# Up weights by column halves, down weights by column quarters, an earlier first release and a shared last norm in a decoder block with 32 experts

## What is computed

```python
x = x + mix @ w_o                       # mix: two attention branches, gated
h = rms_norm(x, norm_ffn_g)
logits = h @ w_router + b_router        # top 4 of 32 experts for each token
g = minimum(h @ w_gate[e] + b_gate[e], 7)
u = clip(h @ w_up[e] + b_up[e], -7, 7)
y += gate * (((u + 1) * g * sigmoid(1.702 * g)) @ w_down[e] + b_down[e])
out = rms_norm(x + y, norm_final_g)
```

## Time and profile before

| | us |
|---|---|
| median of 3 runs (1133.7 to 1134.16) | 1133.88 |
| the profiled execution, its time | 1134.85 |
| the profiled execution, its span | 1133.1 |
| PE busy in it | 1071.8 (95%) |
| DVE, ACT busy | 211.1, 133.4 |
| DMA: 438.16 MB, mean rate | 387 GB/s |
| mean granted clock of TensorE | 0.991 |

### The profile page before, as it was taken

The page is one execution under the profiler, slowest core; times in us unless marked ns, Lnnn a source line. Parts: engine busy times, 40 slices in busy tenths (PEclk is TensorE's granted clock), DMA queues, the critical chain, the costliest instruction groups (busy, mean ns, idle before and its releaser), DMA issues.

```text
span 1133.1 us, 11796 instructions
## 1 busy us (share of the span) xinstructions
PE 1071.8 (95%) x5017; PEld 496.6 (44%) x5017; DVE 211.1 (19%) x507; ACT 133.4 (12%) x227; POOL 7.8 (1%) x17
## 2 busy tenths in 40 slices
PE   9999999999999999999999898989898979998886
PEld 8676888643443434344334332433233324332322
DVE  4132143131211120202021201020202020202021
ACT  1112260110010001000100010001000100010002
POOL 1000000000000000000000000000000000000000
PEclk9999999999999999999999999999999999999998
DMA  9982354599999999999999999999999999999995
GB/s 348 426 326 76 149 223 175 234 372 429 413 425 439 430 426 435 433 427 436 433 427 436 433 427 435 434 427 435 433 428 435 433 428 435 433 422 429 426 429 232
DMA packets 26510, 438.16 MB, mean 387 GB/s; under 512 B 4976, under 2 KB 6256, under 8 KB 8560
## 3 DMA queue, kind: packets, MB, share of 16 engines
q1 hardware_dynamic: 26336, 437.67, 91.2%
q10 hardware_dynamic: 144, 0.07, 0.0%
HBM read 436.28 MB, written 1.05 MB: 386 GB/s over the span
## 4 chain that ended last, share of the span: by engine, by line
PE 63%; DMA 35%; ACT 1%; another core or an unknown queue 1%; issue 0%; DVE 0%; ACTq 0%; DVEq 0%; SPq 0%; POOL 0%; POOLq 0%
DMA ring<-in_experts 35%; PE ps L1492 24%; PE ps L1538 11%; PE ps L1160 9%; PE ps L1408 3%; PE ps L1303 2%; PE ps L1151 2%; PE ps L1547 2%; PE ps L1177 1%; PE ps L1351 1%; PE ps L1348 1%; PE ps L1527 1%; PE ps L1417 1%; ACT region_va L666 0%; PE ps L1194 0%
## 5 line engine op out<-in xcount | busy, mean ns | idle before, releaser
L1492 PE MATMUL ps<-ring,xT 128*64 128x512 f32 x2048 | 458.2, 602 | 26.5 <-DMA ring<-in_experts 26.4
L1492 PEld LDWEIGHTS ps<-ring,xT 128*64 128x64 f32 x2048 | 143.7, 138 | 314.9 <-issue 280.3
L1538 PE MATMUL ps<-ring,region_va 128*64 128x512 f32 x1024 | 229.8, 599 | 25.3 <-DMA ring<-in_experts 13.8
L1538 PEld LDWEIGHTS ps<-ring,region_va 128*64 128x64 f32 x1024 | 73.6, 137 | 159.9 <-issue 126.6
L1160 PE MATMUL ps<-ring 128*128 128x256 f32 x448 | 98.5, 380 | 0.0
L1160 PEld LDWEIGHTS ps<-ring 128*128 128x128 f32 x448 | 84.6, 190 | 12.3 <-issue 0.8
L1056 DVE TENSOR_SCALAR g<-ps 128x1024 f32<-128x1024 f32 x16 | 19.6, 1224 | 349.8 <-PE ps L1492 349.8
L1408 PEld LDWEIGHTS ps<-sel,x 128*128 128x128 f32 x480 | 55.4, 192 | 9.5 <-issue 9.5
L1547 PE MATMUL ps<-g,g_T 128*128 128x512 f32 x128 | 59.2, 605 | 0.0
L1408 PE MATMUL ps<-sel,x 128*128 128x128 f32 x480 | 56.7, 276 | 0.0
L1003 DVE TENSOR_TENSOR xT<-ps,g_ffn 128x512 f32<-128x512 f32 x30 | 20.8, 692 | 193.0 <-PE ps L1408 193.0
(11 more groups left out here) (204 smaller groups left out, 446.8 us busy)
## 6 DMA issues: line engine op xcount, KB each, us to landing
ring<-in_experts SPq DMA_DIRECT2D x72, 4096.0 KB, 46.2
ring<-in_experts SPq DMA_DIRECT2D x41, 2048.0 KB, 47.7
ring<-in_head SPq DMA_DIRECT2D x13, 2048.0 KB, 16.0
ring<-in_experts SPq DMA_DIRECT2D x14, 1024.0 KB, 8.2
ring<-in_first SPq DMA_DIRECT2D x7, 384.0 KB, 6.2
x<-in_x SPq DMA_DIRECT2D x2, 512.0 KB, 24.7
out<-x SPq DMA_DIRECT2D x4, 256.0 KB, 2.7
ring<-in_norm_final_g SPq DMA_DIRECT2D x1, 512.0 KB, 13.0
```

What stands on the lines that cost most here:

```text
L1492: last = mm(bank(banks + half)[rows, :], xT[:, 2 * m + c, rows], w[:, c, k, half * W512:(half + 1) * W512], start=False, stop=m == 3 and c ...
L1538: last = mm(bank(first + half)[rows, :], hTm[:, 2 * m + c, rows], w[:, c, k, half * W512:(half + 1) * W512], start=m == 0 and c == 0, stop ...
```

## The change

**Up** loads now hold four chunks of the contraction and half the columns: 4 and 5 are the left half, 6 and 7 the right half. `up_half` goes. The first transposes move from after the last up load to before it, and those of the gates to after load 4.

**Down** loads hold all eight chunks and a quarter of the columns. `down` multiplies by 256 columns; copies and scatters go by quarters (four copies of 256 columns, eight scatter matmuls of 256), each some loads behind its quarter. In an even pair the gather is cut in two by the last scatter. `down_done` goes.

**Early releases.** w_o's right half is laid out as two column quarters, and the left half of slot 5 is loaded when the first of them has been used (`early_left`). Load 0 of pair 1 starts with a quarter, released after the first column half of chunk 0 (`early_quarter`). Gather chunk 3 moves from before gate load 0 into its middle. Gate loads are laid out by chunk and column half.

**Last load** of all: three quarters and one quarter, in place of two halves.

**Last norm.** Both left halves are added, squared and summed and multiplied by the gain on DVE, before the last scatter; then the right halves: squares and roots on ACT, the rest on DVE. POOL scales the left half of token half 0, ACT that of half 1, which ACT also stores. The table of the root is loaded before the last copies. Three stores: 512 KB and twice 256 KB.

```diff
@@ SP: last load, first releases
+LAST_COL = 3 * SLOT_COLS // 4
-                for c, loaded in enumerate((last_rows, unit_loaded[UNITS - 1])):
+                for lo, hi, loaded in ((0, LAST_COL, last_rows), (LAST_COL, SLOT_COLS, unit_loaded[UNITS - 1])):
...
-                                sp_.wait_ge(first_rows_used, p + 1)
-                                load_columns(row, p, 0, SLOT_COLS // 2, early_half[p])
+                                if p == 0:
+                                    sp_.wait_ge(first_rows_used, 1)
+                                    load_columns(row, p, 0, SLOT_COLS // 4, early_quarter)
+                                sp_.wait_ge(first_rows_used, p + 2)
+                                load_columns(row, p, 0 if p else SLOT_COLS // 4, SLOT_COLS // 2, early_half[p])
...
+                if SLOT_OF[p] == 5:
+                    sp_.wait_ge(wo_done, 3)
+                    load_columns(p // 2, p, 0, SLOT_COLS // 2, early_left)
+                    sp_.wait_ge(wo_done, 4)
+                    load_columns(p // 2, p, SLOT_COLS // 2, SLOT_COLS, slot_loaded[5])
+                    continue
@@ ACT: copies by quarters
-                    for b in range(2):
...
-                        nc.scalar.copy(o_s[:, b * W512:(b + 1) * W512], bank(first + b)).then_inc(o_ready, 1)
+                    if closing and q == PAIRS_PER_ITER - 1:
+                        load_root_table()
+                    for j in range(4):
+                        act.wait_ge(load_used, it * LOADS_PER_ITER + LOADS_PER_PAIR * (q + 1) + 9 + j)
+                        nc.scalar.copy(o_s[:, j * T:(j + 1) * T], bank(first + j % 2)[:, (j // 2) * T:(j // 2 + 1) * T]
+                                       ).then_inc(o_ready, 1)
@@ PE: one pair
+                    for m in range(4):
+                        gate(m)
+                    biases(q, 1, second)
+                    up(0, 0)
+                    transpose_gates()
+                    up(0, 1)
+                    up(1, 0)
                     transpose_hidden(0)
+                    up(1, 1)
+
+                    pe.wait_ge(gt_ready, n + 1)
+                    if q == 1 and not last_pair:
+                        pe.wait_ge(sel_ready, n + 2)
+                        gather(first, range(KC))
+
+                    w = down_weights(0)
+                    pe.wait_ge(hT_ready, n * 2 + 1)
                     if q == 1 and not last_pair:
                         pe.wait_ge(xT_ready, n * 2 + 4)
+                    down(0, w, (0, 1))
+                    if q == 1:
+                        transpose_hidden(1)
+                    down(0, w, (2, 3))
+                    if q == 0:
+                        transpose_hidden(1)
+                    pe.wait_ge(hT_ready, n * 2 + 2)
+                    down(0, w, range(4, KC)).then_inc(load_used, 1)
                     if last_pair:
+                        scatter(0)
+                    w = down_weights(1)
+                    down(1, w, range(KC)).then_inc(load_used, 1)
+                    if last_pair:
+                        scatter(1)
+                    else:
+                        scatter(0)
+                    w = down_weights(2)
+                    down(2, w, range(KC)).then_inc(load_used, 1)
+                    if not last_pair:
+                        scatter(1)
+                    w = down_weights(3)
+                    if last_pair:
+                        down(3, w, range(6))
                         pe.wait_ge(unit_loaded[UNITS - 1], (n + 1) * 16)
+                        down(3, w, range(6, KC)).then_inc(load_used, 1)
                     else:
+                        down(3, w, range(KC)).then_inc(load_used, 1)
+                    scatter(2)
                     if q == 0:
+                        pe.wait_ge(sel_ready, n + 2)
+                        gather(first, range(4))
+                        scatter(3)
+                        gather(first, range(4, KC))
+                    else:
+                        scatter(3)
@@ DVE, POOL, ACT: last norm
+            for a in range(NT):
+                add_experts(a, 0)
+            for a in range(NT):
+                left_squares(a)
...
+            for a in range(NT):
+                nc.vector.tensor_tensor(xg[:, a, :], x3[:, a, 0:W512], gfin[:, 0:W512], ALU.mult).then_inc(fin_g, 1)
+            for a in range(NT):
+                add_experts(a, 1)
...
+            nc.gpsimd.tensor_scalar(x3[:, 0, 0:W512], xg[:, 0, :], rstd[:, 0:1], None, ALU.mult).then_inc(fin_left0, 1)
...
+            nc.scalar.activation(x3[:, 1, 0:W512], xg[:, 1, :], ACT.Copy, scale=rstd[:, 1:2]).then_inc(fin_left1, 1)
+            act.wait_ge(fin_left1, 1)
+            act.dma_start(out_d[P:T, 0:W512], x3[:, 1, 0:W512]).then_inc(stored, 16)
```

More of the change, by code:

```diff
@@ L500, in _ @@
             assert own.n == 5
[L502 to L506 removed]
+            pool.wait_ge(fin_g, 1)
+            pool.wait_ge(rstd_ready, 1)
+            nc.gpsimd.tensor_scalar(x3[:, 0, 0:W512], xg[:, 0, :], rstd[:, 0:1], None, ALU.mult).then_inc(fin_left0, 1)
         @block.scalar
@@ L681, in _ @@
+            rounds_after_first(act, expert_iteration, closing=load_root_table)
             for a in range(NT):
[L682 to L686 removed]
@@ L690, in _ @@
                                      bias=fin_bias[:, a:a + 1]).then_inc(fin_std, 1)
-            act.wait_ge(rstd_ready, 1)
-            for half in range(2):
-                cols = slice(half * W512, (half + 1) * W512)
-                act.wait_ge(fin_g, half + 1)
-                nc.scalar.activation(x3[:, 0, cols], xg[:, cols], ACT.Copy,
-                                     scale=rstd[:, 0:1]).then_inc(fin_done0, 1)
+            act.wait_ge(fin_g, 2)
+            act.wait_ge(rstd_ready, 2)
@@ L1497, in gate_or_up @@
-                                if first_pair and 4 * which + m < HALVED and (c, half) == (0, 1):
-                                    last.then_inc(first_rows_used, 1)
-                            last.then_inc(load_used, 1)
-                            if which == 1 and m == 1:
-                                transpose_gates()
+                                    last = mm(bank(first + half)[rows, :], xT[:, 2 * m + c, rows], w[:, c, half, k, :],
+                                              start=False, stop=m == 3 and c == 1, skip_group_check=True)
@@ new lines, in gate, with up @@
+                                if first_pair and c == 0 and (half == 1 or m == 0):
+                                    last.then_inc(first_rows_used, 1)
+                        last.then_inc(load_used, 1)
+                    def up(half, side):
+                        m = 4 + 2 * half + side
+                        w = loaded(m).rearrange("p (c k n) -> p c k n", c=4, k=2)
+                        for c in range(4):
+                            for k in range(2):
+                                rows = slice(k * SLOTS, (k + 1) * SLOTS)
+                                last = mm(bank(second + half)[rows, :], xT[:, 4 * side + c, rows], w[:, c, k, :],
+                                          start=False, stop=side == 1 and c == 3, skip_group_check=True)
+                            if first_pair and m < HALVED and c == 1:
+                                last.then_inc(first_rows_used, 1)
+                        last.then_inc(load_used, 1)
@@ L1510, in expert_iteration @@
                     pe.wait_ge(oh_ready, n + 1)
-                    def gather_next():
-                        pe.wait_ge(sel_ready, n + 2)
-                        gather(first, range(KC))
-                    gate_or_up(0, first)
-                    gate_or_up(1, second)
-                    pe.wait_ge(gt_ready, n + 1)
-                    if q == 1 and not last_pair:
-                        gather_next()
                     def transpose_hidden(b):
@@ L1529, in transpose_hidden, with down @@
                         last.then_inc(ht_done, 1)
-                    transpose_hidden(0)
+                    def down(j, w, chunks):
+                        out = bank(first + j % 2)[:, (j // 2) * T:(j // 2 + 1) * T]
+                        for c in chunks:
+                            for k in range(2):
+                                rows = slice(k * SLOTS, (k + 1) * SLOTS)
+                                last = mm(out[rows, :], hTm[:, c, rows], w[:, c, k, :], start=c == 0, stop=c == KC - 1,
+                                          skip_group_check=True)
+                        return last
@@ L1532, in expert_iteration @@
+                    w = down_weights(0)
+                    pe.wait_ge(hT_ready, n * 2 + 1)
                     if q == 1 and not last_pair:
                         pe.wait_ge(xT_ready, n * 2 + 4)
-                    def down(w, m, half, c):
-                        for k in range(2):
-                            rows = slice(k * SLOTS, (k + 1) * SLOTS)
-                            last = mm(bank(first + half)[rows, :], hTm[:, 2 * m + c, rows],
```

(7 more changed lines are left out.)

231 lines of the change are left out of this document (99 added, 132 removed).

## The result

| us | before | after |
|---|---|---|
| median of 17 runs each | 1134.08 | 1136.89 |
| ratio | | 1.0024 [1.0018, 1.0031] |
| profiled execution: time, span | 1134.85, 1133.1 | 1136.68, 1134.9 |

The kernel became slower by 2.8 us (2.0 to 3.5), a little over the bound of 0.2% that the prediction set for no change. I had forecast 1132.9, so the error is 4.0 us.

What follows compares the result with a forecast made beforehand. The prediction took the DMA weight stream as the bound, leaving its start at the 297.26 us issue and what follows its last byte. Terms +0.4 - 1.8 + 0.5 = -0.9 us from 1133.88 gave 1132.9, range 1131.0 to 1135.0.

Steps and rivals of the forecast that it cites:

- the pinned issue: Weight load issued at 297.26 us, when PE has used pair 1's first two loads; claimed to fix the stream's start.
- T: Landing of the last weight load, 1119.5 us before the change; forecast within 1 us of 1119.9.
- The early releases at 0 for the stream: Head: loading slot 5's left half and a quarter load sooner gains nothing, since PE's path holds the later issue.
- In steady state even +3 us a pair would stay under: Expert loop: 3 us more PE work a pair stays hidden under the stream's 58.4 us.
- +0.4 us for the stream's start: PE's path up to the issue at 297.26 us grows by 0.4 us, bounds -0.5 and +1.4, delaying the stream equally.
- E' = T+4.2: Tail: PE's last scatter ends 4.2 us after the last landing instead of 6.0, saving 1.8 us.
- My rival of landings that fall differently: Stream's end: code fetches miss the last loads, the last landing comes 1.4 to 1.5 us sooner, 1131.4; chance 0.17.
- +0.5: Last norm and stores: the span ends 8.1 us after the last scatter instead of 7.6; bounds -0.3 and +0.9.
- The clock in the tail: Rival: half-speed PE clock after 1109 us is no longer hidden by a wait, costing 1.6 us: 1134.5; chance 0.15.
- The loop stays in PE's instruction memory: Rival claimed the opposite: the grown loop body overflows and refetches each pass, about 1135.6 to 1136.5; chance 0.06.
- Weight loads are hidden: Rival claimed the opposite: down steps take 0.27 us, +3.5 us at the stream's start, +1.7 at the end, 1138; chance 0.05.
- The pin did not give way: Rival claimed the opposite: up to 1.4 us of the early gain survives the issue at 297 us, 1131.5; chance 0.07.

Runs made afterwards that it cites:

- 16 us in the loop: The kernel before with three gather chunks done twice in six of the eight iterations: 1134.56 us, ratio 1.0002.
- the scatters later: The changed kernel with the last pair's scatters 0 and 1 one load later: 1136.54 us, ratio 1.0019.
- the kernel without it: The changed kernel without PE's code for further rounds (experts with more than 64 tokens), so without the jump past it: 1136.10 us, ratio 1.0015.
- doubled matmuls: The kernel before with the head's four matmuls that put the experts' biases into Y issued twice: 1135.27 us, ratio 1.0007.
- the split unit: The 4.19 MB transfer issued at 297.26 us released in two halves: 1132.94 us (0.9984) on the kernel before, 1135.19 us (1.0006) on the changed one.

## Why the prediction was wrong

**Right: what bounds it.** The stream's start at one issue, and what follows its last byte. 822.0 to 822.35 us lie between the pinned issue and T in eight of the eleven profiles with an unsplit unit, 822.6, 822.9 and 823.5 in the other three. T is the last of 16 landings, that of the slowest engine: half the landings of the last load have come 820.1 to 820.4 us after the pinned issue in all eleven, the last 1.8 to 3.1 us behind that, and it is this lag that makes T late in the three. The early releases at 0 for the stream were right (1136.48 without them), and so was "In steady state even +3 us a pair would stay under" (16 us in the loop at a ratio of 1.0002).

**The step "+0.4 us for the stream's start" failed.** It measured +1.3, counted from the gather's first record, near my upper bound of 1.4. I had priced the down steps (+0.2, measured 0), and the gather's chunk (+0.2 net, measured +0.6: 0.8 in gate load 0, less 0.2 ahead of it), and the scatters not at all: as many columns, so the same time. They measured +0.7; each detour from column tiles to full width and back costs 0.35 us, and the rows that I had read showed scatters at the end only, once a pair. The term at fault is the change of tiling, which I put at nothing without a reason, in a place where 1 us of PE is 1 us of time.

**The step "E' = T+4.2" failed.** It measured T+5.6, 1.4 us later. The step rests on "copies and scatters of quarters 0 and 1 go into PE's waits for loads", and those waits were gone. The issues of down load 8 and their landings, before:

```profile
1053.72 4.24 SPq L403 DMA_DIRECT2D ring<-in_experts  x1
...
ring<-in_experts SPq DMA_DIRECT2D x1, 2048.0 KB, 49.5
```

and after:

```profile
1054.30 4.24 SPq L406 DMA_DIRECT2D ring<-in_experts  x1
...
ring<-in_experts SPq DMA_DIRECT2D x1, 2048.0 KB, 51.5
```

It lands at 1103.2 before, T-16.2, and at 1105.8 after, T-14.7, which is when PE starts on it; the 1.29 us put down to "issue" are that wait. Before, 6.4 us passed from landing 8 to landing 9, with a fetch of code in 1106 to 1108, and PE waited 2.01 us for load 9. After, the same 1.5 us had been lost ahead of load 8, and the landings 8 to 11 come 4.9 us apart. So PE has everything from 1105.86 on, and its chain sets E: four loads of 3.5 to 3.6, 0.6 of transposes, two waits of 0.47 for ACT's copies, scatters of 1.06, 1.06 and 1.99, in all 20.2 us. With a scatter and its copy a load takes PE 5.1 us, more than the 4.9 between landings, so there is no wait left to hide them in.

The other kernels bear it out. E comes 20.3 us after landing 8 in all seven profiles that have the changed kernel's order of the last loads, and in the one where load 8 lands 0.26 us further ahead of T than in the changed kernel (early releases taken back, T-14.96), E is 0.26 us nearer to T (5.33 in place of 5.59). With the scatters later it is 0.2 less, and waits for landings take over; the other 1.2 us to my T+4.2 hang, as I read these rows, on when load 8 lands, and no run has it land at T-16.2 with the changed order. My rival of landings that fall differently came true, but inside the tail and not at its end, and I had looked at T alone.

The 1.5 us of the kernel before are one engine's: of the 16 landings of load 9, 15 stand as those of load 8 did, 4.9 us on, and one comes 1.46 us behind them, at 1109.59, with the fetch at 1107.0 between. A fetch in 1112 to 1114 of the changed kernel moves one engine by 1.5 us as well, but one that stays 0.2 us ahead of the last, and so moved nothing. That the fetch is what holds the engine is still read from the coincidence in time; no run takes this fetch out.

**The step "+0.5" for the norm and the stores failed by 0.8 us.** The parts: the 512 KB store at E+3.87 (predicted E+3.2), the last one at E+4.27 (E+4.2), GpSimd 2.03 us (I took 1.0, with 1.27 as the upper bound from the earlier trace rows), stores bound by bytes (right). What was missing is the fetch for PE's jump: 1.05 us, shown by the kernel without it. It falls on one of 16 engines (one landing of 16 late, above), and the stores' end is that of the last engine. A finish that is faster for PE brings its jump nearer to the stores; nothing in my sum had that. The remaining 0.2 to 0.3 us go with the 0.6 us by which the first store, ACT's at E+3.36, is later after E than before.

**The rivals.** The clock in the tail fell to the 1.2 GHz level before (0.60 in 1109 to 1113) and not after (1.00), nor in any of the eight variants of the changed kernel. The reason is open: of the kernel before and its variants it fell in two of the three with a wait for load 9 of 1.8 to 2.05 us (doubled matmuls: 0.79 in 1109 to 1113), and not in the third, the unchanged one run again (wait 1.80). Where it fell, T to E is 6.04 and 6.19 us, elsewhere 5.79 to 5.86; so 0.2 to 0.4 us of it got past the wait for load 10, and of the -0.3 from T to E a part is the clock's. The loop stays in PE's instruction memory: the view of 450 to 990 us lists no fetch, and 25 are in the whole span. (By "Runtime: NRT & Kernel Launch", section Instruction fetch mechanics, of the Trainium skill, PE has room for 2048 instructions; the trace agrees, with a body of an estimated 1300.) Weight loads are hidden: 2048 of 137 ns under steps of 0.22 us. The pin did not give way.

**Sum.** Predicted +0.4 - 1.8 + 0.5 = -0.9; measured +1.3 - 0.3 + 1.3 = +2.3 by the profiles, 2.8 by the medians. Of the error of 4.0 us these three terms are 0.9, 1.5 and 0.8; 0.3 is the start of the sum (a median of three runs, 1133.88, where seventeen give 1134.08, and the rounding down). The last 0.5, between profiles and medians, is within what single profiles vary by, and stays open; so does why the start of the gather varies by 0.9 us. Not tried: the kernel before without PE's rounds, the split unit without the early releases, and a norm by quarters behind the last scatter.

## What to carry to other kernels

Where a stream of transfers is the bound, look for the one issue that pins it, and ask first whether that transfer can be cut and released in parts: that one edit gave 1.3 us, where the reordering of PE's work cost 1.3. Count the changes between column-tiled and full-width matmuls on the path to it: each there-and-back cost 0.35 us with no column more. And follow a tail back to the landing from which PE has no wait: moving work into a later wait pays only if that wait is still there. Look at the 16 landings of a transfer one by one where its time matters: the last of them alone decides.

## What the hardware showed that I had not expected

A fetch of 16 KB of code for a jump over code that never runs added 1.05 us to the end of the stores, because it falls among them and makes one engine of 16 late (E to end 7.78 without it, 8.6 to 9.1 with it in the eight others of this form). GpSimd's multiplication of 128x512 by a value for each partition took 2.03 us, more than its two-input form at 1.27. SP's issue of a DMA takes 0.35 us at 298.34 and 4.24 us at 1076.99, where the landing is 43.5 us away, so a semaphore that SP waits for late in the stream can have less to say than the queue has. A distant landing alone doesn't make it long: the last issue of the kernel before took 0.43 us, with its landing 48.6 us away.
